# The rotary turn of the first attention's queries: read from PSUM shifted by 64 partitions on VectorE, in place of a matmul with a constant matrix

## What is computed

```python
q = (h @ w_q[j]).reshape(B, T, N_HEADS, HEAD_DIM)      # T = 256, 8 heads of 128
q = rope(rms_norm(q, q_norm[j]), cos, sin).transpose(0, 2, 1, 3)
att = moba_attention(q, k_blocks, v_blocks, k_mean)    # causal softmax over the 256 keys
y = att.transpose(0, 2, 1, 3).reshape(B, T, D) @ w_o[j]

def rope(x, cos, sin):                                 # half = 64
    x1, x2 = xf[..., :half], xf[..., half:]
    return concatenate([x1 * c - x2 * s, x2 * c + x1 * s])
```

## Time and profile before

| | |
|---|---|
| time, median of 3 runs | 1318.75 us (1318.58 to 1319.08) |
| span of the profiled execution | 1317.1 us |
| PE busy | 1266.0 us, 96% of the span |
| DVE busy | 1080.4 us, 82% |
| ACT busy | 632.3 us, 48% |
| POOL busy | 186.3 us, 14% |
| PE's share of the chain that ended last | 88% |

### The profile page before, as it was taken

How to read it: one execution, slowest core, us unless ns; L and a number is a source line. 1 busy time by engine, 2 the same in 40 slices (tenths; PEclk the granted TensorE clock), 3 DMA queues, 4 the chain that set the end, 5 groups by cost and what they waited for, 6 DMA issues and landing times.

```text
span 1317.1 us, 26714 instructions
## 1 busy us (share of the span) xinstructions
PE 1266.0 (96%) x10588; PEld 1231.7 (94%) x10588; DVE 1080.4 (82%) x1684; ACT 632.3 (48%) x996; POOL 186.3 (14%) x205
## 2 busy tenths in 40 slices
PE   2999999999999999999999999999999999999996
PEld 1999999899999889999999999999999889999996
DVE  6998988898878777989878778999976888895674
ACT  3534344444343555554346653433366465455453
POOL 4598900000000000000001000000001014530000
PEclk8999999999999999999999999999999999999999
DMA  9999887399888369988953389887666499555561
GB/s 367 380 329 309 304 306 271 130 323 334 310 305 287 116 206 365 331 291 306 315 199 101 125 253 336 297 305 247 216 195 181 74 190 178 167 157 188 173 196 49
DMA packets 110893, 319.76 MB, mean 243 GB/s; under 512 B 24096, under 2 KB 35776, under 8 KB 110528
## 3 DMA queue, kind: packets, MB, share of 16 engines
q1 hardware_dynamic: 110784, 318.25, 72.9%
HBM read 313.19 MB, written 5.01 MB: 242 GB/s over the span
## 4 chain that ended last, share of the span: by engine, by line
PE 88%; DVE 7%; ACT 3%; issue 1%; DMA 1%; SPq 0%; ACTq 0%; DVEq 0%
PE tiles L376 18%; PE tiles L378 18%; PE tiles L377 18%; PE acc L376 8%; PE acc L378 8%; PE acc L377 8%; PE nrm L552 2%; DVE arena L1483 1%; PE tiles L578 1%; PE tiles L595 1%; DVE w_lo L368 1%; PE tiles L580 1%; ACT w_hi L364 1%; DVE arena L1438 1%; DMA x<-in_x_t 1%
## 5 line engine op out<-in xcount | busy, mean ns | idle before, releaser
L364 ACT CAST w_hi<-land 128x1024 fp32r<-128x1024 f32 x391 | 408.2, 1047 | 446.3 <-PE tiles L378 277.8
L368 DVE TENSOR_TENSOR w_lo<-land,w_hi 128x1024 fp32r<-128x1024 f32 x391 | 485.8, 1249 | 141.3 <-ACT w_hi L364 140.1
L376 PE MATMUL tiles<-x_hi,w_hi 128*128 128x256 f32 x1384 | 393.5, 284 | 0.8 <-DVE arena L1889 0.5
L377 PE MATMUL tiles<-x_lo,w_hi 128*128 128x256 f32 x1384 | 391.6, 283 | 0.0
L378 PE MATMUL tiles<-x_hi,w_lo 128*128 128x256 f32 x1384 | 391.6, 283 | 0.0
L376 PEld LDWEIGHTS tiles<-x_hi,w_hi 128*128 128x128 f32 x1384 | 265.3, 192 | 3.0 <-issue 1.0
L377 PEld LDWEIGHTS tiles<-x_lo,w_hi 128*128 128x128 f32 x1384 | 265.4, 192 | 0.1
L378 PEld LDWEIGHTS tiles<-x_hi,w_lo 128*128 128x128 f32 x1384 | 265.3, 192 | 0.0
L1438 DVE SCALAR_TENSOR_TENSOR arena<-arena 128x1024 f32<-128x1024 f32 x184 | 227.3, 1239 | 11.7 <-ACT arena L1171 8.3
L376 PE MATMUL acc<-h_hi,w_hi 128*128 128x256 f32 x704 | 199.3, 283 | 0.0
L377 PE MATMUL acc<-h_lo,w_hi 128*128 128x256 f32 x704 | 199.2, 283 | 0.0
(11 more groups left out here) (342 smaller groups left out, 1626.4 us busy)
## 6 DMA issues: line engine op xcount, KB each, us to landing
land<-in_stream SPq DMA_DIRECT2D x391, 512.0 KB, 4.6
arena<-in_gstream SPq DMA_DIRECT2D x184, 512.0 KB, 6.5
w_dram<-arena SPq DMA_DIRECT2D x3, 512.0 KB, 6.4
arena<-w_dram SPq DMA_DIRECT2D x6, 256.0 KB, 9.2
arena<-in_c_rows SPq DMA_DIRECT2D x2, 512.0 KB, 5.2
x<-in_x_t SPq DMA_DIRECT2D x1, 1024.0 KB, 9.9
arena<-in_ssm_bn SPq DMA_DIRECT2D x1, 1024.0 KB, 8.1
u_dram<-arena SPq DMA_DIRECT2D x1, 1024.0 KB, 5.3
```

Source lines behind the costliest of these rows:

```text
L364: nc.scalar.copy(w_hi[:, u % RING], land[:, u % LAND]).then_inc(hi_done, 1)
L368: nc.vector.tensor_tensor(w_lo[:, u % RING], land[:, u % LAND], w_hi[:, u % RING].bitcast(F32), ALU.subtract).then_inc(lo_done, 1)
L376: nc.tensor.matmul(outs, lh, rh, start=first, stop=False, **kw)
L377: nc.tensor.matmul(outs, lh, rl, start=False, stop=False, **kw)
```

## The change

`q_rot` and the matrix `rot1` are gone, with the semaphore `q_rotd`. The product with the sine table now reads `qacc[h]` as `q_unit(h)` left it, in two VectorE operations of 64 partitions each: the upper half of the head goes to the lower half of `q_sin` and the other way round. Since the gain `q_norm` has not been applied in PSUM, each is a `scalar_tensor_tensor` that multiplies by it and by the sine table; the sign moved into the table's second half. In place of `q_rotd` they wait for `q_sqd`, ACT's last read of the head. The constants `cons` lose 128 columns. POOL's part, ACT's part, the sum and all other orders stay.

```diff
-for _name, _n in [("eps", 1), ("ident", 128), ("ones", 128), ("rot1", 128), ("rot2", 96), ("cos1", T), ("sin1", T),
+for _name, _n in [("eps", 1), ("ident", 128), ("ones", 128), ("rot2", 96), ("cos1", T), ("sin1", T),
@@ PE
-            def q_rot(h):
-
-                pe.wait_ge(q_out, h + 1)
-                pe.wait_ge(q_sqd, h + 1)
-                nc.tensor.matmul(qacc[h], con("rot1", P), qT[:, h], start=True, stop=True).then_inc(q_rotd, 1)
-
@@ PE, order: every call of q_rot goes
             first_units(UNIT["q"], qacc[0:3], x_hi, x_lo, KT * 5)
-            q_rot(0)
             q_unit(3)
-            q_rot(1)
-            q_rot(2)
             scores1(0)
             q_sum(0)
             q_unit(4)
-            q_rot(3)
             scores1(1)
...
             for h in range(2):
                 q_unit(5 + h)
-                q_rot(4 + h)
                 scores1(2 + h)
...
             q_unit(7)
-            q_rot(6)
             scores1(4)
             values1(2)
             q_sum(1)
-            q_rot(7)
             pe.wait_ge(q_roots, 2)
@@ DVE
             def q_rope(h):
-                dve.wait_ge(q_rotd, h + 1)
-                V.tensor_tensor(q_sin[:, h % 2], qacc[h], sin1, ALU.mult).then_inc(q_sind, 1)
+                dve.wait_ge(q_sqd, h + 1)
+                for a, b in ((0, 64), (64, 0)):
+                    m = V.scalar_tensor_tensor(out=q_sin[a:a + 64, h % 2], in0=qacc[h][b:b + 64],
+                                               scalar=vec("q_norm")[b:b + 64], in1=sin1[b:b + 64],
+                                               op0=ALU.mult, op1=ALU.mult)
+                m.then_inc(q_sind, 1)
@@ constants
-    put("sin1", np.tile(np.sin(ang), (2, 1)).astype(np.float32))
+    put("sin1", np.concatenate([np.sin(ang), -np.sin(ang)]).astype(np.float32))
```

More of the change, by code:

```diff
@@ L297, in build_program @@
         k_scaled, k_roped, k_turn, kT_done = sem("k_scaled"), sem("k_roped"), sem("k_turn"), sem("kT_done")
-        q_out, q_sqd, q_rotd, q_cosd = sem("q_out"), sem("q_sqd"), sem("q_rotd"), sem("q_cosd")
+        q_out, q_sqd, q_cosd = sem("q_out"), sem("q_sqd"), sem("q_cosd")
         q_sind, q_roped, q_sums, q_roots, q_scales = (sem("q_sind"), sem("q_roped"), sem("q_sums"), sem("q_roots"),
@@ L2193, in constants @@
     put("ones", np.ones((P, P), np.float32))
-    for name, first, half in (("rot1", 0, 64), ("rot2", 64, 16)):
-        m = np.zeros((P, P if name == "rot1" else QK_2), np.float32)
+    for name, first, half in (("rot2", 64, 16),):
+        m = np.zeros((P, P), np.float32)
         for i in range(half):
@@ L2198, in constants @@
             m[first + i, first + half + i] = 1.0
-        put(name, m[:m.shape[1]] if name == "rot2" else m)
+        put(name, m[:, 0:QK_2])
     pos = np.arange(T, dtype=np.float32)
```

## The result

| | before | after |
|---|---|---|
| time, median | 1318.75 us (1318.58 to 1319.08) | 1323.7 us (1323.15 to 1324.6) |
| ratio to before | | 1.0038, 95% interval 1.0026 to 1.005 |
| span of the profiled execution | 1317.1 us | 1321.4 us |
| DVE busy | 1080.4 us | 1085.0 us |
| `o_rows(0)` starts, from the start of DVE's split of query unit 4 | 29.73 us | 32.68 us |

I had forecast 1320.2 us, at most 1322.8. The sign of the mechanism was right, its size was not: PE does wait for VectorE, and `o_rows(0)` starts 2.95 us late in place of 1.42; and PE's clock falls on top, which I had given 4%.

A forecast was written before the change was run, and what follows sets the result against it. In the query-turn stage PE was taken to wait for VectorE's list, so the 3.4 us of matmuls removed return as waiting and o_rows(0) comes 1.42 us late: 1318.75 + 1.4 = 1320.2 us, range 1318.6 to 1322.8.

The forecast's parts named there:

- The sign of the mechanism: At o_rows(0): PE, 3.4 us ahead by its own list, waits for DVE and starts 1.42 us late.
- What bounds: Query-turn stage: PE is full behind it but already waits 0.97 us for DVE's sine product before o_rows(0).
- Cost of a turn, 1.48 us: DVE's q_rope per head: two shifted products and the sum, 0.68 us more than before, 5.4 us for eight.
- late starts read from rows 7: DVE instructions changing partitions, in profile rows 7: starts 0.12 us late behind a split, 0.09 late for the next.
- The walk, 1.42 us: DVE, ACT and PE followed from 705.80 us: o_rows(0) starts at 735.81 in place of 734.39.
- POOL ... stays hidden: GpSimd waits later for q_roped, but its cosine product is needed one head later, so it costs nothing.
- the 0.67 again: DVE's normalise_head to the next q_rope keeps its 0.67 us as before.
- Granted clock, "I keep 1.00": PE's clock in the stage stays at 1.00, as it did with 0.97 us idle in 6.40, 15%.
- rival (d): PE's clock falls to half in its waits; about 5 us of it gives 1325 us; chance 0.04.
- Rival (a): DVE's shifted products cost like any other; only head 7's 0.45 us reaches o_rows(0): 1319.2 us; chance 0.20.
- Rival (c): DVE's shifted products run at half pace, 0.52 us per head, 4.2 for eight: 1324.3 us; chance 0.16 with milder forms.
- Range: Whole kernel: 1318.6 to 1322.8 us, upper end taking half of the half-pace price and leaving out the clock's fall.

The follow-up runs named there:

- c: Kernel before with its matmul kept, the sine product done twice on VectorE, once into a place nothing reads; 1319.3 us, ratio 1.0000.
- b: Changed kernel with only one unshifted product per head on all 128 partitions, halves not swapped; 1317.8 us, ratio 0.9988.
- a: Changed kernel with both products of each head unshifted on all 128 partitions, halves not swapped; 1321.6 us, ratio 1.0017.
- d: Changed kernel with GpSimd's cosine product, from head 4 on, waiting for normalise_head of four heads earlier; 1322.5 us, ratio 1.0022.
- g: Changed kernel, GpSimd at its old time, PE's waits filled with 4, 2 and 4 matmuls that nothing reads; 1321.55 us, ratio 1.0019.
- i: Changed kernel with heads 2 to 7 turned on GpSimd, its products delayed, plus 2 filling matmuls before turn1(0); 1318.3 us, ratio 0.9992.
- e: d plus matmuls that nothing reads in PE's waits: 3 before turn1(0), 2 before the second root, 4 before o_rows(0); 1320.3 us, ratio 1.0007.

## Why the prediction was wrong, step by step

- **What bounds.** Right: VectorE's list sets `o_rows(0)`, and every microsecond taken from PE came back as waiting. c and b show it from both sides: 2.3 us of added work on VectorE are free, and without added work the removal brings 2.0 us on the way to `o_rows(0)`.
- **Cost of a turn, 1.48 us.** Right to a few hundredths, with the late starts read from rows 7 (1.26 behind a split, 0.98 for the pair); its terms as written add up to 1.47. a against the change shows 0.11 us for each instruction that goes over to other partitions. By the Trainium skill (VectorE: DVE Perf Modes, section "Two Vector instructions with no wait between them") an instruction whose input or output starts in another group of 32 partitions than the last one in that memory starts only when every earlier one has finished. The trace agrees: in the change the first product starts at 705.37, 0.03 us behind the end of the split (704.11 + 1.23).
- **The walk, 1.42 us.** The step that failed is "POOL ... stays hidden" with "the 0.67 again" for `normalise_head`. I asked when GpSimd's result is needed, not when it now starts and what it then runs beside. Measured: 2.95 us as it was, 1.28 with GpSimd out of the way. The other steps held: in d the product of head 6 starts 25.22 us behind the split's start, where the walk had 25.35 (729.89 + 0.12 - 704.66), and PE waits 1.35 us at `turn1(0)`, where it had 1.4.
- **Granted clock, "I keep 1.00".** Failed, and by the medians is the larger term. I had set the share of idle time beside a stretch of 15%, and put the rival (d) at 4% with a price of 5 us. It came true with 6.8 us of half clock, of which only what fell on `o_rows(0)` cost: 1.35 us in the profile, 2.3 to 2.6 us of the medians. The price had to be worked out from what PE does in those microseconds, its chance from the many waits that the walk itself had listed.
- **Rival (a), 1319.2 with 0.45 us late at `o_rows(0)`.** In a it was 0.39 early. The walk held DVE until ScalarE's `out_hi(2)`; but ScalarE had waited there for `q_unit(7)`, and PE was now ahead, so that DVE had no wait there. The time was 2.4 us above its before all the same, through the clock.
- **Rival (c), half pace.** Wrong: 0.483 us on 64 partitions, 0.476 on 128.
- **Range.** Its upper end, 1322.8, counted (d) as out. Two terms on the same side, each with its own mechanism, gave 1323.7. As worked out the ends are 1319.2 - 0.4 = 1318.8 and 1320.2 + 2.1 + 0.2 = 1322.5, not 1318.6 and 1322.8; the measured time lies outside of either.

What stays open: why the clock fell at 734.4 us in a too, where PE waited less than in the change, and why near 710 us in a, g and i but not in the change, whose PE list is the same up to there as g's. The traces show the falls behind the 1-column matmuls of `q_sum` or behind waits, and e shows that the one at 732 us can be undone by filling; which of the two counts how much wasn't separated.

## What to carry to other kernels

Taking work from the engine with the longest busy time pays only as far as the engine that takes it over has room in that stage. Find that room in microseconds first (here 2.3 were free, and the change brought 5.4). If an engine gets ahead, all that it releases starts sooner: for each such start, look what now runs beside it. And where the walk makes PE wait in several pieces, price a fall of its clock over the PE work behind the waits.

## What the runs showed that I had not expected

- Two `tensor_scalar` on float32 in SBUF take 0.93 to 0.99 us in place of 0.55 while GpSimd runs one `tensor_tensor` of 256 columns, and DVE's sum of two SBUF operands 0.54 to 0.57 in place of 0.42; DVE's products out of PSUM beside the same GpSimd instruction keep their length (0.42 us before).
- A `scalar_tensor_tensor` with a constant takes 0.42 us and starts 0.33 behind its like, with a column of scalars 0.48 and 0.39.
- GpSimd's shifted product of 64 partitions takes 0.64 us, as long as its unshifted one of 128.
- PE's clock can fall to half without a wait in front of it: in g PE was busy for 3.43 of the 3.50 us up to 709.5, and the clock fell at 709.8, behind 16 matmuls of one column. In the change the same list ran through at full clock.
